# The memory's keys first in the stream, its mean and the decays' logarithms later, a shorter lookahead: the opening of a two-block transformer kernel on one Trainium2 core

## What is computed

```python
mod_l = c_act @ ada_w[i] + ada_b[i]                 # modulation: shift, scale, gate
h_l = _rms_norm(x, norm_gain[i]) * (1 + sc_l[:, None]) + sh_l[:, None]
lg_f = jax.nn.log_sigmoid(logit_f.astype(jnp.float32))   # decays of the retention heads
v = _heads(p[..., 2 * RET_QK_W:2 * RET_QK_W + RET_V_W], RET_HEADS, RET_DV)
mkv = jnp.einsum('bmd,de->bme', mem_n, w_mem_kv[layer])  # keys and values of the memory
```

## Time and profile before

| | |
|---|---|
| median of 3 runs | 3294.51 us (3293.44 to 3294.83) |
| the profiled execution's own time | 3294.67 us |
| its span, first to last instruction | 3293.3 us |
| PE busy | 3202.9 us (97%) |
| DVE busy | 1757.5 us (53%) |
| ACT busy | 1294.8 us (39%) |
| end of the part that the change touches | 215.6 us into the span |

### The profile page before, as it was taken

How to read it: one execution, slowest core, us unless ns; L and a number is a source line. 1 busy time by engine, 2 the same in 40 slices (tenths; PEclk the granted TensorE clock), 3 DMA queues, 4 the chain that set the end, 5 groups by cost and what they waited for, 6 DMA issues and landing times.

```text
span 3293.3 us, 48422 instructions
## 1 busy us (share of the span) xinstructions
PE 3202.9 (97%) x20546; PEld 2776.4 (84%) x20546; DVE 1757.5 (53%) x2569; ACT 1294.8 (39%) x1859; POOL 0.2 (0%) x4
## 2 busy tenths in 40 slices
PE   7999999999999999999997999999999999999998
PEld 6677777877778787777875789988999999999998
DVE  5543444434444444444436567778776665555555
ACT  4443223232322323222234455556554444444443
POOL 0000000000000000000000000000000000000000
PEclk9999999999999999999998999999999999999999
DMA  9854433233332333323234334444655554565564
GB/s 369 299 203 166 173 109 134 96 109 135 115 122 103 115 109 135 122 102 138 91 111 165 106 119 144 151 141 152 199 172 167 176 170 154 183 195 193 195 195 149
DMA packets 153927, 508.98 MB, mean 155 GB/s; under 512 B 15344, under 2 KB 35952, under 8 KB 152944
## 3 DMA queue, kind: packets, MB, share of 16 engines
q1 hardware_dynamic: 149328, 493.03, 43.5%
q10 hardware_dynamic: 4384, 12.85, 1.0%
HBM read 501.62 MB, written 4.19 MB: 154 GB/s over the span
## 4 chain that ended last, share of the span: by engine, by line
PE 91%; DVE 4%; ACT 2%; DMA 1%; issue 1%; ACTq 0%; DVEq 0%
PE bank L580 29%; PE bank L582 28%; PE bank L581 28%; PE bank L642 3%; PE bank L826 1%; DMA raw<-stream 1%; PE bank L807 1%; DVE w_lo L1612 1%; PE bank L817 1%; PE bank L658 0%; ACT w_hi L1047 0%; ACT a_s L1332 0%; DVE a_s L1982 0%; DVE a_numbers L1989 0%; PE bank L751 0%
## 5 line engine op out<-in xcount | busy, mean ns | idle before, releaser
L580 PE MATMUL bank<-h_hi,w_hi 128*128 128x256 f32 (+1 forms) x4032 | 1260.7, 313 | 10.7 <-DVE w_lo L1612 10.2
L582 PE MATMUL bank<-h_hi,w_lo 128*128 128x256 f32 (+1 forms) x4032 | 1240.0, 308 | 0.0
L581 PE MATMUL bank<-h_lo,w_hi 128*128 128x256 f32 (+1 forms) x4032 | 1239.6, 307 | 0.0
L1612 DVE TENSOR_TENSOR w_lo<-raw,w_hi 128x1024 fp32r<-128x1024 f32 x729 | 881.1, 1222 | 579.9 <-ACT w_hi L1047 575.5
L1047 ACT ACTIVATE w_hi<-raw 128x1024 fp32r<-128x1024 f32 x729 | 761.2, 1057 | 898.1 <-PE bank L582 568.9
L580 PEld LDWEIGHTS bank<-h_hi,w_hi 128*128 128x128 f32 x4032 | 759.1, 188 | 83.4 <-issue 35.4
L581 PEld LDWEIGHTS bank<-h_lo,w_hi 128*128 128x128 f32 x4032 | 759.6, 188 | 45.3 <-issue 3.6
L582 PEld LDWEIGHTS bank<-h_hi,w_lo 128*128 128x128 f32 x4032 | 759.4, 188 | 43.7
L580 PE MATMUL bank<-w_hi,h_hi 128*128 128x512 f32 x704 | 287.4, 408 | 24.3 <-DVE w_lo L1612 14.9
L582 PE MATMUL bank<-w_hi,h_lo 128*128 128x512 f32 x704 | 278.1, 395 | 0.0
L581 PE MATMUL bank<-w_lo,h_hi 128*128 128x512 f32 x704 | 278.0, 395 | 0.0
(11 more groups left out here) (251 smaller groups left out, 2880.4 us busy)
## 6 DMA issues: line engine op xcount, KB each, us to landing
raw<-stream SPq DMA_DIRECT2D x904, 512.0 KB, 4.2
raw_h<-stream SPq DMA_DIRECT2D x32, 512.0 KB, 9.3
res<-tokens_in ACTq DMA_DIRECT2D x4, 1024.0 KB, 8.7
vg<-mem_in ACTq DMA_DIRECT2D x4, 512.0 KB, 9.0
h_hi<-mem_kv ACTq DMA_DIRECT2D x2, 1024.0 KB, 11.1
out<-res SPq DMA_DIRECT2D x4, 512.0 KB, 3.0
mem_kv<-qk ACTq DMA_DIRECT2D x1, 1024.0 KB, 7.8
mem_kv<-vg ACTq DMA_DIRECT2D x1, 1024.0 KB, 6.9
```

Of the source, the lines that this page charges most:

```text
L580: pe.matmul(out, sh, mh, start=start, stop=False, **checks)
L581: pe.matmul(out, sh, ml, start=False, stop=False, **checks)
L582: return pe.matmul(out, sl, mh, start=False, stop=stop, **checks)
L1612: dve.tensor_tensor(in_quarters(m.low(raw)[:, :]), m.raw[SLOT[raw]], in_quarters(m.w_hi[slot][:, :]).bitcast(F32), ALU.subtract).then_inc( ...
```

## The change

1. The three modulation chunks ahead of the keys are gone; the stream begins with the first key chunk. The same 64 chunks are laid out anew: 16 beside the keys, 12 and 12 beside the two passes of memory values (before 12 and 15), then 5, 5, 5, 5 and 4 in the first head's value stage (before 5, 5, 4, 4, after the 6 that followed the last memory chunk).
2. The squares of the memory are taken apart from the tiles' scaling. They come behind the first key chunks (`MEM_SQUARES`), and the mean beside the third tile (`(n, half) == (2, 0)`). DVE takes tiles 0 and 1 of the keys out of PSUM only then (`key_out`).
3. PE waits for the memory's activations tile by tile, no longer for eight at once, and for the conditioning after the first chunk. The first two chunks are split after tiles 3 and 7.
4. The logarithms, with their Exp, move to the first chunk of the memory's values.
5. `weights_to` looks two chunks ahead, no longer four, in the second pass of memory values and in `("v", 0)`.

```diff
+MEM_SQUARES = {(0, 0): range(0, 5), (0, 1): range(5, 10), (1, 0): range(10, KT)}
...
 BESIDE = {"start": modulation_beside(
-    [(("begin",), 3)]
-    + [(("mk", i, j), 1) for i in range(8) for j in range(2)]
-    + [(("mv", 0, c), 1 + c % 2) for c in range(8)]
-    + [(("mv", 1, c), n) for c, n in enumerate((1, 1, 1, 2, 1, 2, 1, 6))]
-    + [(("v", i), n) for i, n in enumerate((5, 5, 4, 4, 0, 0, 0, 0))],
+    [(("mk", i, j), 1) for i in range(8) for j in range(2)]
+    + [(("mv", i, c), 1 + c % 2) for i in range(2) for c in range(8)]
+    + [(("v", i), n) for i, n in enumerate((5, 5, 5, 5, 4, 0, 0, 0))],
...
@@ tensor_program
             for k in range(first, first + 8):
+                if what == ("mk", 0):
+                    pe.wait_ge(*s["h_lo"].at("mem", k))
...
-            if (n, half) == (0, 1):
+            if (n, half) == (0, 0):
+                pe.wait_ge(*s["cond_done"].at())
+            if (n, half) == (2, 0):
                 memory_means()
...
@@ scalar_program
-        square("mem", k, (sq_out(k, SIDE), m.mem_raw[:, k, :]))
-        if k == 7:
-            weights_to(WHERE["mk", 0][0], 1)
+        if k in (3, 7):
+            weights_to(WHERE["mk", 0][0], 1 + k // 4)
...
             weights_to(WHERE["mk", n][half], 2 if n == 0 else SLOTS)
-            if (n, half) == (0, 1):
+            for k in MEM_SQUARES.get((n, half), ()):
+                square("mem", k, (sq_out(k, SIDE), m.mem_raw[:, k, :]))
+            if (n, half) == (2, 0):
                 root(("mean", "mem"), s["meaned"].at("mem"), m.rstd[:, SIDE])
...
-            weights_to(WHERE["mv", n][c])
+            weights_to(WHERE["mv", n][c], SLOTS if n == 0 else 2)
             if n == 0:
                 if c == 0:
                     tokens_in(3)
+                    act.wait_ge(*s["dve_step"].at("logit"))
+                    act.activation(m.lt[1][:, :], m.lt[0][:, :], ACT.Exp).then_inc(*s["cond_act"].up("logit"))
...
-        weights_to(WHERE["v", 0][c])
+        weights_to(WHERE["v", 0][c], 2)
...
@@ vector_program
+            for k in MEM_SQUARES.get((n, half), ()):
+                add_square("mem", k, SIDE)
+            if (n, half) == (2, 0):
+                reciprocal(("mean", "mem"), m.rstd[:, SIDE], ("mem",))
+                reciprocal(("mem_means",), m.mem_rstd[:, :], ("mem_means",))
+                dve.wait_ge(*s["rstd"].at("mem"))
+                key_out(0)
+                key_out(1)
+            if half == 1 and n >= 2:
+                key_out(n)
             beside("start", "mk", n, half)
     for n in range(2):
         for c in range(8):
-            weights_to(WHERE["mv", n][c])
+            weights_to(WHERE["mv", n][c], SLOTS if n == 0 else 2)
             if n == 0:
+                if c == 0:
+                    logarithms()
...
-        weights_to(WHERE["v", 0][c])
+        weights_to(WHERE["v", 0][c], 2)
```

More of the change, by code:

```diff
@@ L150, in beside @@
             ada(layer, n, (c,))
-    beside("start", "begin")
     for n in range(8):
@@ L592, in tile @@
                 banks.drop(*what)
-            if what == ("mk", 0):
-                pe.wait_ge(*s["h_lo"].at("mem", first + 7))
             if what == ("wo", 0):
@@ L688, in keys_beside @@
         return between
-    pe.wait_ge(*s["cond_done"].at())
-    beside("start", "begin")
     for n in range(8):
@@ L1146, in x0_squares @@
             square("x0", k, (sq_out(k, BOTH), m.res[:, k, :]))
-    weights_to(WHERE["mk", 0][0], 2)
-    beside("start", "begin")
     for n in range(8):
@@ L1692, in vector_program @@
     dve.tensor_scalar(m.cond[:, :, 0:2], m.cond_t[:, :, :], 0.5, None, ALU.mult).then_inc(*s["cond_done"].up())
[L1695 to L1716, removed]
-    dve.tensor_tensor(lt[3], lt[3], lt[0], ALU.mult).then_inc(*step.up())
-    dve.wait_ge(*step.now())
-    dve.scalar_tensor_tensor(out=m.lg[:, :], in0=logit, scalar=0.0, in1=lt[3], op0=ALU.min, op1=ALU.add
-                             ).then_inc(*step.up())
-    dve.wait_ge(*step.now())
-    dve.tensor_scalar(m.nlg[:, :], m.lg[:, :], -1.0, None, ALU.mult).then_inc(*step.up("nlg"))
-    dve.memset(m.ones_mean[:, :], 1.0 / D_MODEL)
-    dve.memset(m.ones_dv[:, :], 1.0 / RET_DV)
     dve.tensor_scalar(m.half_gain[:, :], m.param("ret_gain"), 0.5, None, ALU.mult).then_inc(*s["tables_set"].up())
@@ L1728, in vector_program, with logarithms @@
     i.then_inc(*step.up("bias1"))
+    def logarithms():
+        logit = m.param("logit")
+        lt = [x[:, :] for x in m.lt]
+        dve.tensor_scalar(lt[0], logit, -1.0, None, ALU.mult).then_inc(*step.up())
+        dve.wait_ge(*step.now())
+        dve.tensor_tensor(lt[0], lt[0], logit, ALU.min).then_inc(*step.up("logit"))
+        dve.wait_ge(*s["cond_act"].at("logit"))
+        dve.tensor_scalar(lt[0], lt[1], 2.0, None, ALU.add).then_inc(*step.up())
+        dve.wait_ge(*step.now())
+        dve.reciprocal(lt[0], lt[0]).then_inc(*step.up())
+        dve.wait_ge(*step.now())
+        dve.tensor_tensor(lt[0], lt[0], lt[1], ALU.mult).then_inc(*step.up())
+        dve.wait_ge(*step.now())
+        dve.tensor_tensor(lt[2], lt[0], lt[0], ALU.mult).then_inc(*step.up())
+        dve.wait_ge(*step.now())
+        dve.tensor_scalar(lt[3], lt[2], 1.0 / (2 * LOG1P_TERMS - 1), None, ALU.mult).then_inc(*step.up())
+        for n in range(LOG1P_TERMS - 2, 0, -1):
+            dve.wait_ge(*step.now())
+            dve.scalar_tensor_tensor(out=lt[3], in0=lt[3], scalar=1.0 / (2 * n + 1), in1=lt[2], op0=ALU.add, op1=ALU.mult
+                                     ).then_inc(*step.up())
+        dve.wait_ge(*step.now())
+        dve.tensor_scalar(lt[3], lt[3], 1.0, -2.0, ALU.add, op1=ALU.mult).then_inc(*step.up())
+        dve.wait_ge(*step.now())
+        dve.tensor_tensor(lt[3], lt[3], lt[0], ALU.mult).then_inc(*step.up())
+        dve.wait_ge(*step.now())
+        dve.scalar_tensor_tensor(out=m.lg[:, :], in0=logit, scalar=0.0, in1=lt[3], op0=ALU.min, op1=ALU.add
+                                 ).then_inc(*step.up())
+        dve.wait_ge(*step.now())
+        dve.tensor_scalar(m.nlg[:, :], m.lg[:, :], -1.0, None, ALU.mult).then_inc(*step.up("nlg"))
     dve.wait_ge(*step.at("bias1"))
@@ L1737, in vector_program, with key_out @@
                                  ).then_inc(*s["h_lo"].up("mem", k))
-        add_square("mem", k, SIDE)
-        if k == 7:
-            weights_to(WHERE["mk", 0][0], 1)
-    weights_to(WHERE["mk", 0][0], 2)
-    beside("start", "begin")
+        if k in (3, 7):
+            weights_to(WHERE["mk", 0][0], 1 + k // 4)
+    def key_out(n):
+        done(("mk", n))
+        dve.tensor_tensor(m.mem_k[:, n, :], psum("mk", n)[:, LAT], m.rstd[:, SIDE], ALU.mult).then_inc(*banks.up("mk", n))
     for n in range(8):
@@ L1745, in vector_program @@
             weights_to(WHERE["mk", n][half], 2 if n == 0 else SLOTS)
-            if half == 1:
-                done(("mk", n))
-                if n == 0:
-                    reciprocal(("mean", "mem"), m.rstd[:, SIDE], ("mem",))
-                    reciprocal(("mem_means",), m.mem_rstd[:, :], ("mem_means",))
-                    dve.wait_ge(*s["rstd"].at("mem"))
-                dve.tensor_tensor(m.mem_k[:, n, :], psum("mk", n)[:, LAT], m.rstd[:, SIDE], ALU.mult
-                                  ).then_inc(*banks.up("mk", n))
+            for k in MEM_SQUARES.get((n, half), ()):
[8 more added lines that the diff above has]
+                key_out(n)
             beside("start", "mk", n, half)
```

4 lines of the change are left out of this document (2 added, 2 removed).

## The result

| | before | after |
|---|---|---|
| median | 3293.03 us (20 runs, 3287.76 to 3296.64) | 3297.86 us (20 runs, 3293.74 to 3301.64) |
| ratio | | 1.0016 (95%: 1.0010 to 1.0021) |
| profiled execution: own time, span | 3294.67, 3293.3 us | 3295.94, 3294.6 us |
| last value chunk of the first head ends | 215.57 us | 216.90 us |

A forecast was written before the change was run, and what follows sets the result against it. PE was taken as the bound (91% of the span), so only its idle time and lost clock counted: -4.5 + 3.6 - 1.7 = -2.6 us from 3294.67 gave 3292.1 us, own range 3288.5 to 3296, with rivals 3286.4 to 3297.5.

The forecast's parts named there:

- start: Kernel's opening up to the 42.3 us point: PE begins its first key chunk earlier, 4.5 us gained.
- tokens' mean: Behind the tokens' mean: DVE's reciprocal delays a split, 1.9 us of wait plus 1.7 us of clock, 3.6 us lost.
- value stage: First head's value stage: 15.0 us of idle and lost clock become 13.3, a gain of 1.7 us.
- that rival: Start: its gain is none, PE merely runs into the stream earlier; 4.5 us come back, 3296.6 us; chance 0.13.
- the lookahead of two does all it is for: Value stage rival: chunks 5 and 6 land before ACT asks; the block after the fourth goes, 3283.8 us; chance 0.08.
- now ACT is not held: First value chunk: already split, banks free, so PE waits only for two low parts, 0.9 us of idle.
- Rounds 1 and 2: Value stage, each a value chunk plus five modulation chunks: forecast to run through without a wait.
- just in time: Value stage rounds: the split ends between 0.3 us late and 0.2 us early for PE.
- the fourth rival: Slower: value chunks late in every round, chunks 1, 2 and 4 paying 3.7 us each, 3303 us; chance 0.07.
- Round 3: Value stage: the 1 MB store shares the rings, split 2.1 us late plus 1.7 us of clock, 3.8 us.
- The block behind value chunk 4: ACT stands on landings for chunks 5 and 6: turn waits 1.2 us, then 4.4 us idle and 2.7 us clock.
- The last chunk: End of the first head's value stage: the last value chunk waits 0.3 us.

The follow-up runs named there:

- look4_store0: Changed kernel with the lookahead of four back in both places and the memory's store issued at the value stage's first chunk: 3289.04 us, ratio 0.9990.
- all3: Changed kernel with store at the stage's first chunk, lookahead of four back, no value-chunk splits inside the modulation parts there: 3282.67 us, ratio 0.9968, 5 runs.
- before_store0_nopart: Kernel before with the store at the value stage's first chunk and no splits inside the modulation parts there: 3286.97 us, ratio 0.9987.
- before_look2: Kernel before with only the lookahead of two, in the memory values' second half and first head's value stage: 3293.81 us, ratio 1.0005.
- look4: Changed kernel with the lookahead of four back in the memory values' second half and the first head's value stage: 3294.00 us, ratio 1.0006.
- before_store0: Kernel before with the memory values' store moved one chunk earlier, to the value stage's first chunk: 3290.86 us, ratio 0.9996.
- store0: Changed kernel with the 1 MB store of the memory's values issued at the value stage's first chunk, not the second: 3291.67 us, ratio 0.9998.
- store3: Changed kernel with the memory's store two chunks later, at the value stage's fourth chunk: 3289.87 us, ratio 0.9997.
- nopart: Changed kernel without ACT's splits of value chunks inside the modulation parts in the first head's value stage: 3290.58 us, ratio 0.9996.
- mv4: Changed kernel with the lookahead of four back in the second half of the memory's values alone: 3294.95 us, ratio 1.0011.

## Why the prediction was wrong

I compare at three points of PE: the modulation chunk that the prediction had at 42.3 us, the last memory chunk, and the last value chunk. They lie at 42.28, 142.96 and 215.57 us before, 40.42, 141.01 and 212.65 us in its second trace, and 36.20, 139.20 and 216.90 us after. Before, three modulation chunks more lie ahead of the first point, one fewer and two fewer in the stretches behind (0.43 us each).

| term | forecast | first trace of before | second trace of before |
|---|---|---|---|
| start | -4.5 | -4.8 | -2.9 |
| tokens' mean | +3.6 | +1.9 | +2.0 |
| value stage | -1.7 | +4.2 | +5.2 |
| sum | -2.6 | +1.3 | +4.3 |

The last column is the one that the medians (+4.8 us) bear out.

- **The start: right in mechanism, and sized on an unusual trace.** PE's first key chunk came at 10.94 us (forecast 11.3), the idle before the third at 2.07 us (2.7) with 1.7 us of clock, the point itself at 36.2 (36.5). What failed is the other side, "the same point lies at 42.3 us before". Of that, 1.6 us were half clock behind the 1.71 us wait, which one trace of five shows, and 0.2 us a later first landing. What is left of the gain is a lasting gain, not time that PE only reached earlier: `look4_store0`, the comparison of `all3` with `before_store0_nopart`, and the stretch 42.3 to 118 us without idle speak against that rival.
- **The tokens' mean: wait right, clock wrong.** Forecast 1.9 us of wait, and 1.7 of clock because 1.9 lies "above the 1.71 us that cost the clock". The wait was 1.91 us. In the five traces that have it at this place the clock stayed at 2.4 GHz; in `before_look2`, behind a wait just as long, the next chunk took 1.3 us longer.
- **The lookahead of two** brings nothing in the value stage (`look4`, `before_look2`); the 0.9 us that I forecast before the first value chunk (1.28 measured) are there with either lookahead (1.25 in `look4`). My rival that "the lookahead of two does all it is for" falls, and so does the reason "now ACT is not held".
- **Rounds 1 and 2** ran through in the first trace after, as forecast (0 us). In the second, round 2 waited 1.42 us: "just in time" was near enough, and the fourth rival, 2 us late and half clock in every round, did not come.
- **Round 3: the step that failed.** "Two more chunks' worth of bytes in the queue make the split 2.1 us late, and 1.7 us of clock follow: 3.8 us." By the ends of the chunks it cost 7.7 us: 1.84 us of wait for a modulation chunk and 2.92 for the split, where 2.1 was forecast, and 2.9 us of clock (0.34 x 8.6) for 1.7. The store put the chunks off by 4.9 us, not 2.6: that two chunks' worth of bytes is all it costs was wrong. In the old kernel, issued at 174.44 us, it cost at most little (1.2 us by `before_store0`, not clear of noise); so the change pays for a store that it does not touch. `store0` and `store3` give 5.8 and 7.6 us back (5.8 and 7.0 against their groups).
- **The block behind value chunk 4: right in mechanism and size.** Forecast 8.3 us (1.2 for the turn, 4.4 for the split, 2.7 of clock); by the ends of the chunks 8.7, split 2.46 and 1.80 us of idle and the rest half clock, 0.50 from 193 to 196 us. ACT was idle on a landing ahead of it, as I wrote, and `nopart` shows the cause. That the size fits is in part luck: the pieces were others in the second trace, and `nopart` gives back 6.2 of the 8.7 us, as a wait of 1.74 us then stands before value chunk 6.
- **The last chunk** 0.7 us for 0.3. The value stage's loss is so 1.3 + 7.7 + 8.7 + 0.7 = 18.4 us (19.3 by idle and clock) against 13.3.

From -2.6 to +4.8 us it is 7.4 us. By the last column 1.6 of them are the start's baseline and 6.9 the value stage (3.9 of these by round 3), less 1.6 at the mean: 6.9 us. The other 0.5 us are within what the medians can tell.

## What to carry to other kernels

When a change brings a stage forward, list the transfers that it does not touch and ask among which others they now fall. A large store between loads that are just in time can cost more than its bytes, as it did here, and the wait can take the matmul engine's clock on top. Before a loss in one trace is booked as a gain, look at a second execution: a wait followed by half clock in one was followed by none in the next. And where an engine serves two orders of work, a helper that splits far ahead "on the way" (here inside `ada_part`) can stand on a landing while the short work that others need waits behind it: 6.9 us from one condition.

## What the runs showed of the hardware

- **The length of a wait of 1.1 to 2.5 us does not tell whether the clock is lost.** PE ran at 2.4 GHz behind waits of 1.51 us (second trace of before, 24.86 us), 1.71 us (the same, 190.11 us) and 1.91 us (tokens' mean, five traces). It ran at 1.2 GHz behind 1.71 us (25.07 us, first trace of before), behind 1.91 us (`before_look2`), and even behind 1.08 us (`store0`, before the turn at 183.82 us, mean clock 0.59 from 183.8 to 187.9 us). In two traces of one program the turn's wait of 2.46 us was followed by half clock, one of 2.28 us by none. Before the third key chunk PE waited 2.33 us in `all3` and in `look4_store0`, and the clock from 22.9 to 26.1 us was 1.00 and 0.61. All 16 waits of 2.88 us and more between 20 and 216 us in the fourteen traces were followed by half clock: the value chunk behind took 7.1 to 8.6 us, not 5.7, and behind the one before a turn (`mv4`) four modulation chunks took 3.6 us, not 1.9. The Trainium skill ("TensorE: Matmul & The Clock Gate", HAM oscillation) has pieces of matmuls between DMA waits of some 3 to 5 us start cold each time. The long waits here agree. The prediction took it as a rule for waits of about 2 us too, of which the section does not tell, and the rows above show both outcomes.
- **A table load had no drain behind it.** The load for the Exp began at 76.21 us, took 1.28 us, and the Exp started at 77.51 us; the `part` ahead of it had ended at 76.20:

```profile
75.83 0.37 ACT L1078 ACTIVATE part<-bank 128x256 f32<-128x256 f32 x1
76.21 1.28 ACT L1165 ACT_TABLE_LOAD   x1
77.51 0.22 ACT L1165 ACTIVATE lt<-lt 128x16 f32<-128x16 f32 x1
```

  The Trainium skill ("ScalarE: Activation LUTs", What ACT_TABLE_LOAD costs) counts 2.66 us for a switch. The rows leave no room for more than the load itself. The load at 33.57 us in the same trace is alike: `part` ends at 33.55 us, the load takes 1.28 us, and the root starts at 34.86 us.
- **A 1 MB store slowed the rings in one place and not in another**: 256 against 378 GB/s at 157.7 us, but 393 GB/s at 181.2 us and 421 at 174.4 us. The slow 4.4 us came in all five traces with the store at that place, and hardly any of the store's own bytes ran in them. `before_store0`, with its store issued at 146.9 us, has them too (288 GB/s, none of the store's bytes), and `before_store0_nopart` (147.1 us) less markedly (330 GB/s, 0.09 MB). No run tells why.
